# First group's z from the unscaled input, and the state-space rounds rearranged

## The reference, cut to what matters

```python
u = rmsnorm(h, mix_norm)
z   = in_cols(u, w_in, 5)                                    # 2048 wide
xbc = silu(causal_conv(in_cols(u, w_in, 6), conv_w, conv_b)) # 4 taps; x 2048, B 1024, C 1024
dt  = softplus(in_cols(u, w_in, 7) + dt_bias)                # 32 heads
# 8 groups, 4 heads each, head width 64, state 128, chunks of 64 tokens; da = dt * a
cum = cumsum(da); seg = cum[t] - cum[s]; decay = exp(where(s <= t, seg, -inf))
cb = C B^T; y = (cb * decay) (x*dt) + exp(cum) * (C state)
state = exp(cum_last) * state + B^T (x * dt * exp(cum_last - cum))
y = (y + D * x) * silu(z)
y = rmsnorm(y) per group of 256 channels, * ssm_norm         # then the branch's output matrix
```

## Time and profile before

| | |
|---|---|
| median of 3 runs | 1847.29 us (1846.7 to 1848.17) |
| profiled execution | 1847.36 us |
| its span, first to last instruction | 1845.5 us |
| TensorE busy (matmuls) | 98% |
| VectorE, ScalarE, GpSimd busy | 53%, 33%, 8% |
| granted TensorE clock, mean | 0.995 of full speed |

### The profile page before, as it was taken

The page is one execution under the profiler, slowest core; times in us unless marked ns, Lnnn a source line. Parts: engine busy times, 40 slices in busy tenths (PEclk is TensorE's granted clock), DMA queues, the critical chain, the costliest instruction groups (busy, mean ns, idle before and its releaser), DMA issues.

```text
span 1845.5 us, 26225 instructions
## 1 busy us (share of the span) xinstructions
PE 1806.9 (98%) x9852; PEld 1508.4 (82%) x9852; DVE 977.6 (53%) x1376; ACT 610.7 (33%) x942; POOL 145.1 (8%) x116
## 2 busy tenths in 40 slices
PE   7999999999999999999999999999999999999997
PEld 5888888878888888788988888887888888888885
DVE  6444443379888888732444445545334544444333
ACT  4323222233333344332233334443222422323221
POOL 4111100031111111100000000000000011111000
PEclk9999999999999999999999999999999999999998
DMA  4323223322222222132222222222222322223331
GB/s 154 103 93 100 93 101 103 110 84 70 73 74 69 68 68 68 58 103 91 92 69 82 90 87 82 84 78 89 95 99 91 103 92 92 101 92 101 103 105 66
DMA packets 47352, 164.91 MB, mean 89 GB/s; under 512 B 5520, under 2 KB 6672, under 8 KB 47296
## 3 DMA queue, kind: packets, MB, share of 16 engines
q1 hardware_dynamic: 43584, 158.10, 26.1%
q10 hardware_dynamic: 3712, 6.03, 1.0%
HBM read 162.01 MB, written 2.10 MB: 89 GB/s over the span
## 4 chain that ended last, share of the span: by engine, by line
PE 70%; issue 21%; DVE 6%; POOL 1%; ACT 1%; DMA 0%; DVEq 0%; POOLq 0%; ACTq 0%; SPq 0%
PE G L534 33%; PE G L576 12%; PE I L534 9%; PE G L550 7%; DVE WL L1443 2%; DVE CV L1626 1%; PE I L896 1%; POOL hid L456 1%; PE I L930 1%; PE I L906 1%; PE I L704 1%; PE I L712 1%; PE G L761 1%; DVE UL L1459 1%; DVE un L1581 1%
## 5 line engine op out<-in xcount | busy, mean ns | idle before, releaser
L1443 DVE TENSOR_TENSOR WL<-RAW,WH 128x1024 fp32r<-128x1024 f32 x297 | 387.9, 1309 | 298.2 <-ACT WH L1025 290.2
L1025 ACT CAST WH<-RAW 128x1024 fp32r<-128x1024 f32 x297 | 309.6, 1048 | 230.9 <-PE I L534 126.2
L534 PE MATMUL G<-UH,WH 128*128 128x512 f32 x696 | 172.8, 390 | 0.0
L534 PE MATMUL G<-UH,WL 128*128 128x512 f32 x696 | 171.9, 389 | 0.0
L534 PE MATMUL G<-UL,WH 128*128 128x512 f32 x696 | 171.9, 389 | 0.0
L534 PEld LDWEIGHTS G<-UH,WH 128*128 128x128 f32 x696 | 130.6, 188 | 28.0 <-issue 1.0
L534 PEld LDWEIGHTS G<-UH,WL 128*128 128x128 f32 x696 | 130.6, 188 | 27.1
L534 PEld LDWEIGHTS G<-UL,WH 128*128 128x128 f32 x696 | 130.6, 188 | 27.1
L534 PE MATMUL G<-NH,WH 128*128 128x512 f32 x448 | 113.2, 395 | 1.4 <-ACT SC L1098 1.4
L534 PE MATMUL G<-NL,WH 128*128 128x512 f32 x448 | 110.7, 389 | 0.0
L534 PE MATMUL G<-NH,WL 128*128 128x512 f32 x448 | 110.6, 389 | 0.0
(11 more groups left out here) (299 smaller groups left out, 2477.5 us busy)
## 6 DMA issues: line engine op xcount, KB each, us to landing
RAW<-in_slabs SPq DMA_DIRECT2D x297, 512.0 KB, 3.3
h<-in_x SPq DMA_DIRECT2D x4, 512.0 KB, 6.8
bias<-in_rel ACTq DMA_DIRECT2D x16, 128.0 KB, 3.0
out_y<-h ACTq DMA_DIRECT2D x8, 256.0 KB, 2.2
bias<-in_rel ACTq DMA_DIRECT2D x16, 112.0 KB, 2.6
cst<-in_cst SPq DMA_DIRECT2D x1, 168.0 KB, 3.6
ut<-in_wgk SPq DMA_DIRECT2D x3, 32.0 KB, 8.8
```

What stands on the lines that cost most here:

```text
L534: ins = mm(dst, W[:, n.slot, (k - k0) * P:(k - k0 + 1) * P], R[:, k, :], start=begin and which == 0 and k == k0, stop=end and which == 2 a ...
L1025: nc.scalar.copy(WH[:, n.slot, :], RAW[:, n.slot, :]).then_inc(split_hi, 1)
L1443: V.tensor_tensor(WL[:, n.slot, :], RAW[:, n.slot, :], WH[:, n.slot, :].bitcast(F32), ALU.subtract).then_inc(split_lo, 1)
```

## The change

- Group 0's z tile is computed from UH and UL. ScalarE evicts it with the token's 1/rms as a scale (`raw_z`), takes tanh from SBUF, VectorE gates it there. The sums of dt (`dt_sums`) follow z instead of standing between its third and fourth block, and write to I34.
- NL is made by VectorE (`scaled_lo`), four tiles behind `dt_logits` and four behind `dt_softplus`; `raw_evict` and `conv_begin` of tile 0 stand earlier, and the order of what VectorE and ScalarE do up to group 0's end is new.
- MSH (`da_hi`) and MSL (`da_lo`) read SC directly instead of gsc, and those of group g + 1 are made in round g: MSH behind `conv_silu` of tile 3, MSL behind `intra` of group g.
- XD is made on ScalarE already multiplied by D, in four activations (one a head); XTE and XDT are computed from I01 itself, XTE first, ahead of `lo`. GpSimd's multiplication goes.
- `conv_silu` and `ssm_y` change places: Y stands behind the silu of tile 2. One `hi` moves behind BK's copy, the squares move ahead of tanh 3.
- The squares have 1/256 in their scale; the variance is an addition on GpSimd; ScalarE scales two of Y's four blocks, VectorE two.
- `ssm_intra` takes the two halves of the partitions in turn for each head, instead of four heads of one half, then four of the other.

```diff
@@ GpSimd
             def da_lo(g):
-                pool.wait_ge(sems["group_const"], after("group_const", g))
                 pool.wait_ge(sems["intra_done"], last("intra_done", g - 1))
-                inc(nc.gpsimd.tensor_tensor(MSL[:].rearrange("p (q t) -> p q t", t=CH),
-                                            bc(gsc[:, 28:32, :].rearrange("p j r -> p (j r)"), CH),
-                                            causal[:].unsqueeze(1).to_broadcast([P, TT * HPG, CH]), ALU.mult),
+                inc(nc.gpsimd.tensor_tensor(MSL[:].rearrange("p (j r t) -> p j r t", j=TT, t=CH),
+                                            bc(SC[:, 28:32, bass.ds(HPG * g, HPG)], CH), causal_all, ALU.mult),
                     "da_lo_masked")
             def ssm(g):
-                pool.wait_ge(sems["xte_ready"], after("xte_ready", g))
-                pool.wait_ge(sems["group_norm"], after("group_norm", g))
-                d = ggrp[:, 2:6].unsqueeze(1).unsqueeze(3).to_broadcast([P, TT, HPG, CH])
-                x4 = XD[:].rearrange("p j (r c) -> p j r c", r=HPG)
-                inc(nc.gpsimd.tensor_tensor(x4, x4, d, ALU.mult), "xd_ready")
+                pool.wait_ge(sems["ssm_squares"], last("ssm_squares", g))
...
+                inc(nc.gpsimd.tensor_tensor(var4[:], ss4[:], four_eps[:], ALU.add), "ssm_var")
                 pool.wait_ge(sems["ssm_var"], after("ssm_var", g))
                 inc(nc.gpsimd.tensor_tensor(rstd4[:], var4[:], minus_half[:], ALU.pow), "ssm_rstd")
...
             norm(1)
-            for m in range(KT):
-                pool.wait_ge(uh_ready, 16 + m + 1)
-                nc.gpsimd.tensor_tensor(NL[:, m, :], un[:, m, :], NH[:, m, :].bitcast(F32),
-                                        ALU.subtract).then_inc(ul_ready, 1)
             da_split()
-            with pool.Fori(0, NG) as i:
-                da_lo(i)
+            pool.wait_ge(dt_pool, DA_SPLIT)
+            pool.wait_ge(ul_ready, 24)
+            da_lo(0)
+            with pool.Fori(0, NG - 1) as i:
+                da_lo(i + 1)
                 ssm(i)
+            ssm(NG - 1)
@@ TensorE
                 pe.wait_ge(sems["da_lo_masked"], last("da_lo_masked", g))
+                pe.wait_ge(dt_act, 6)
...
                 pe.wait_ge(sems["xte_ready"], after("xte_ready", g))
+                pe.wait_ge(sems["xdt_ready"], after("xdt_ready", g))
...
             def ssm_intra():
-                for c in range(NCH):
-                    j, s = c // 2, half(c)
+                for j in range(TT):
                     for rr in range(HPG):
-                        ins = mm(I01[s, j * 256 + rr * CH:j * 256 + (rr + 1) * CH], M[s, j, rr, :],
-                                 XDT[s, j, rr * CH:(rr + 1) * CH], start=True, stop=True)
+                        for s in (half(0), half(1)):
+                            ins = mm(I01[s, j * 256 + rr * CH:j * 256 + (rr + 1) * CH], M[s, j, rr, :],
+                                     XDT[s, j, rr * CH:(rr + 1) * CH], start=True, stop=True)
...
+            for j in range(TT):
+                tm_tile(n + 4, wn + 4, j, source=(UH, UL))
+            dt_sums()
             pe.wait_ge(uh_ready, 24)
             pe.wait_ge(ul_ready, 24)
-            for j in range(TT):
-                tm_tile(n + 4, wn + 4, j)
-                if j == 2:
-                    dt_sums()
-            pe.wait_ge(dt_act, 6)
@@ ScalarE
+            def raw_z(n, wn):
+                act.wait_ge(slab_done, n.value + 2)
+                act.wait_ge(norm_rstd, 2)
+                for j in range(TT):
+                    bank = (wn + j // 2).slot
+                    ins = A(ZS[:, j, :], G[:, bank, (j % 2) * 256:(j % 2 + 1) * 256], ACT.Copy, scale=rstd4[:, j:j + 1])
+                    ins.then_inc(z_scaled, 1)
+                    if j % 2:
+                        act.wait_ge(z_scaled, j + 1)
+                        act.sem_inc(g_free[bank], 1)
...
-                inc(nc.scalar.copy(XD[:].rearrange("p j c -> p (j c)"), I01[:]), "x_copied")
+                act.wait_ge(sems["group_norm"], after("group_norm", g))
+                for rr in range(HPG):
+                    ins = A(XD[:, :, rr * CH:(rr + 1) * CH],
+                            I01[:].rearrange("p (j c) -> p j c", j=TT)[:, :, rr * CH:(rr + 1) * CH], ACT.Copy,
+                            scale=ggrp[:, 2 + rr:3 + rr])
+                inc(ins, "x_copied")
...
+            def ssm_scale(g):
+                act.wait_ge(sems["ssm_rstd"], last("ssm_rstd", g))
+                for j in range(TT // 2):
+                    inc(A(Y[:, j, :], Y[:, j, :], ACT.Copy, scale=rstd4[:, j:j + 1]), "ssm_scaled_act")
...
                 hi(n + 5)
+                hi(n + 6)
                 conv_begin(0, 2, n + 2, wn + 2)
                 conv_tanh(0, 1, wn + 1)
-                hi(n + 6)
                 conv_begin(0, 3, n + 3, wn + 3)
+                raw_z(n + 4, wn + 4)
+                hi(n + 7)
+                decay_exps()
+                conv_tanh(0, 2, wn + 2)
+                hi(n + 8)
+                conv_tanh(0, 3, wn + 3)
...
                 for t in range(4):
-                    conv_begin(p, t, n + t, wn + t)
+                    conv_begin(p, t, n + t, wn + t, t > 0)
                     if t == 0:
-                        ssm_copy_exp(inner)
+                        ssm_copy_exp(inner, n + 3)
+                    if t == 3:
+                        ssm_squares(inner)
                     conv_tanh(p, t, wn + t)
-                ssm_squares(inner)
+                ssm_scale(inner)
@@ VectorE
                 lo(At(N_SMALL + 4))
                 raw_evict(1, n + 1, wn + 1)
+                dt_logits()
+                for m in range(4):
+                    scaled_lo(m)
+                conv_taps(0, 0, n, wn)
+                raw_evict(2, n + 2, wn + 2)
+                lo(n + 4)
+                lo(n + 5)
+                dt_reciprocal()
+                conv_silu(0, 0)
+                conv_taps(0, 1, n + 1, wn + 1)
+                raw_evict(3, n + 3, wn + 3)
+                lo(n + 6)
+                dt_softplus()
+                for m in range(4, KT):
+                    scaled_lo(m)
...
                 conv_silu(0, 1)
                 conv_taps(0, 2, n + 2, wn + 2)
-                lo(n + 6)
                 conv_silu(0, 2)
+                dve.wait_ge(dt_pool, DA_SPLIT)
+                da_hi(0)
+                lo(n + 7)
                 conv_taps(0, 3, n + 3, wn + 3)
                 conv_silu(0, 3)
+                dt_to_end()
+                group_scalars(0)
+                lo(n + 8)
...
                 for t in range(4):
                     conv_taps(p, t, n + t, wn + t)
-                    lo(n + t + 3)
                     if t == 0:
                         ssm_x(inner)
+                    lo(n + t + 3)
                     if t == 1:
                         ssm_m(inner)
                         ssm_chain(inner)
-                    if t == 3:
+                    conv_silu(p, t)
+                    if t == 2:
                         ssm_y(inner)
-                    conv_silu(p, t)
+                da_hi(p)
                 ssm_scale(inner)
```

More of the change, by code:

```diff
@@ L565, in fm_fresh, with tm_tile @@
                 ins.then_inc(slab_done, 1)
-            def tm_tile(n, wn, j, thirds=range(3)):
+            def tm_tile(n, wn, j, thirds=range(3), source=(NH, NL)):
                 if j == 0 and thirds[0] == 0:
@@ L652, in dt_sums @@
                 da = SC[:, 0:4, :].rearrange("p j h -> p (j h)")
-                mm(I01[:, T:T + 128], upto_t[:], da, start=True, stop=True)
-                mm(I01[:, T + 128:T + 256], after_s[:], da, start=True, stop=True)
+                mm(I34[:, 0:128], upto_t[:], da, start=True, stop=True)
+                mm(I34[:, 128:256], after_s[:], da, start=True, stop=True)
                 for c in range(NCH):
-                    dst = I2[:, 32 * (c // 2):32 * (c // 2) + 32] if c % 2 else \
-                        I01[:, T + 256 + 16 * c:T + 288 + 16 * c]
-                    ins = mm(dst, ones[half(c), :], SC[half(c), c // 2, :], start=True, stop=True)
+                    o = (T if c % 2 else 256) + 32 * (c // 2)
+                    ins = mm(I34[:, o:o + 32], ones[half(c), :], SC[half(c), c // 2, :], start=True, stop=True)
                 ins.then_inc(dt_pe, 1)
@@ L716, in turn_back @@
             def turn_back(src, dst, ready, g, done):
-                pe.wait_ge(sems[ready], last(ready, g))
+                for name in ready:
+                    pe.wait_ge(sems[name], last(name, g))
                 for f in range(2):
@@ L797, in _ @@
                     0: lambda: ssm_turn(i), 1: lambda: ssm_cb_u(i), 3: lambda: (ssm_inter(i), ssm_intra()),
-                    7: lambda: turn_back(Y, I01, "ssm_scaled", i, "ssm_turned")})
+                    7: lambda: turn_back(Y, I01, ("ssm_scaled", "ssm_scaled_act"), i, "ssm_turned")})
             g = NG - 1
@@ L809, in _ @@
             output_half(n + 3, wn + 3, 0)
```

(23 more changed lines are left out.)

82 lines of the change are left out of this document (40 added, 42 removed).

## The result

The changed kernel took 1851.3 us, the kernel before 1847.18, each the median of 18 runs: a ratio of 1.0021 with an interval of [1.0014, 1.0028]. So it is 4 us slower, where 1836.5 was forecast, and it lies outside the range. One of the 18 runs before took 3666.69 us, which the median does not feel. The profiled execution has a span of 1848.5 us.

A forecast was written before the change was run, and what follows sets the result against it. With TensorE busy for 98% of the span, only its waits, lower-clock stretches and time between matmuls could be won. Terms 1.3 + 6.7 + 1.4 + 1.4 = 10.8 us off the median 1847.29 gave 1836.5, range 1833 to 1840.

The forecast's parts named there:

- rival 4: Y scaled too late, so turn_back stalls 1.8 us in each of 8 groups: 14.5 us, above 1851; chance 0.06.
- Rival 3: turn_back becomes the wait because GpSimd's operations keep VectorE's: 0.3 to 1.2 us a round, 1839 to 1845; chance 0.14.
- rival 5: The waits go and others of the same size come in, so no change; chance 0.02.
- 43.6 to 43.9 named for right: Sign that the forecast is right: the state-space rounds take 43.6 to 43.9 us each.
- Group 0: First state-space group: gap before z goes, a 4.3 us wait comes before XT's transposes; 1.3 us gained, bounds -1.2 and 5.5.
- warm or cold: Group 0: u cannot start before XTE and XDT are ready at 439.8, whether TensorE's clock is full or low.
- the taps could be kept back: Group 0's lower bound of -1.2 us: silu 1 or taps 2 kept back 2.5 us by GpSimd's MSL.
- The rounds: Rounds after group 0: the MSL and XTE waits go, 6 x 1.12 = 6.7 us, bounds 0 and 6.7.
- `turn_back` holds: End of each round: scaled Y ready at 42.5, wanted at 43.15, margin 0.65 us; no stall booked, up to 1.2 a round.
- `intra`: the term: Alternating halves in intra gives back 3 to 4 ns an instruction: 8 x 0.18 = 1.4 us, bounds 0 and 10.5.
- rival 1: The two halves of intra overlap, worth 10.5 us: time 1828.5; chance 0.10.
- The last group: Last state-space group: X products ready 0.7 us earlier, inter 1.2 to 2.2 earlier; 1.4 us gained, bounds 0.5 and 3.

The follow-up runs named there:

- e7: The changed kernel with four_eps in the unused half of minus_half's 32 bytes, so every tensor lies where it lay before the change: 1833.92 us, ratio 0.9925.
- e1: The kernel before with an unused 16-byte tensor where four_eps would stand: 1863.62 us, ratio 1.009.
- e9: e7 with group 0's conv chain put earlier in the queues of VectorE and ScalarE: 1832.47 us, ratio 0.992.
- e8: e7 with intra in its old order, four heads of one half, then four of the other: 1838.94 us, ratio 0.9951.
- e4: The kernel before with the weight buffers WH and WL moved by 32 bytes and everything behind them by 64: 1878.85 us, ratio 1.0173.
- e2: The kernel before with an unused tensor of 64 bytes where four_eps would stand: 1846.06 us, ratio 0.9991.
- e3: The changed kernel with 16 unused bytes behind four_eps, so the tensors behind it move by 64: 1835.24 us, ratio 0.9933.

## Why the prediction was wrong, point by point

**The step that failed** is one that the working did not even list, and so priced at nothing: the tensor `four_eps`, and with it the assumption that matmuls which the change does not touch keep their pace. (The working says it once, of "TensorE's fm ends unchanged until 407.28", and there it held, because those products are on UH and UL.) The trace of before could not show the price, for in it every distance was a multiple of 512. In its place the runs show 17.4 us (e7 against the changed kernel) or 16.2 (e1 against the kernel before), from the distance between the two operands of each matmul. That took the forecast 10.8 us and the 2.5 more that the change brings, and left 4 of loss. The time lies where rival 4 put it, above 1851, but its mechanism is not there: `turn_back` waits in no round. Rival 3 is out for the same reason, and rival 5, no change, because e7 is 13.3 faster. One sign was met by luck: the changed kernel's rounds take 517.23 - 473.54 = 43.69 us, within the 43.6 to 43.9 named for right. There the shorter `intra` made up for the slower matmuls.

The rest is read against e7, where the layout is that of before. Its feed-forward started 0.82 later than before by the trace (258.97 against 258.15), so 0.82 comes off its times. Its timeline in group 0:
```profile
421.16 2.11 PE L536 MATMUL G<-NH,WH 128*128 128x512 f32 x8
...
431.27 1.73 PE L668 MATMUL I<-ident,XT 128*128 128x128 f32 x8 [4.36 <-DVE CT L1703]
...
435.17 2.01 PE L536 MATMUL G<-NH,WH 128*128 128x512 f32 x8
...
440.74 0.69 PE L686 MATMUL I<-CT,BT 128*64 128x64 f32 x16
441.35 1.13 PE L693 MATMUL I<-XTE,BK 64*128 64x256 f32 x8
442.32 1.02 PE L698 MATMUL I<-XTE,BK 64*128 64x256 f32 x6
443.27 2.12 PE L536 MATMUL G<-NH,WH 128*128 128x512 f32 x8
```
**Group 0: right in its waits, 0.8 instead of 1.3.** Round 0 begins at 420.34, forecast 420.35. The stall is 4.36, forecast 4.3. XTE and XDT are there at 439.85, forecast 439.8:
```profile
439.46 1.21 DVE L1725 TENSOR_TENSOR XDT<-I,gsc 128x1024 f32<-128x1024 f32 x1
```
But u comes at 440.53, 0.7 later, and is over at 442.45, where 441.8 to 442.0 was forecast and 443.25 was read before. No wait stands in front of it: TensorE itself was late. From the first transposes to the next fm it took 3.90 us at a clock of 0.54, against 2.27 at the full clock in e9. So the lower clock cost 1.6 us, and the step "warm or cold" was wrong: 0.9 or so went into the time in which u would have waited for XDT, and the other 0.7 were lost.

The conv chain itself kept its forecast, tanh 2 done at 423.58 for 423.6, although raw_z took 1.78 for 1.6 and taps 2, which the walk priced undisturbed at 2.23, ran beside GpSimd's MSL. The row is VectorE's of the changed kernel:
```profile
421.59 3.95 DVE L1684 SCALAR_TENSOR_TENSOR CV<-BT,gconv,CV 128x511 f32<-128x511 f32 x3
```
MSL ran from 421.20 to 423.43 there. That the taps could be kept back was named as a bound; tanh 2 did not wait for them, since ScalarE still had the exponentials to do when they ended.

**The rounds: right.** The chain of e7, with z of rounds 0 and 1:
```profile
456.33 2.01 PE I L707 x64
458.34 11.71 PE G L578 x96
...
501.66 11.71 PE G L578 x96
```
A round takes 501.66 - 458.34 = 43.32 where it took 45.06: 1.74 less, of which 0.61 is `intra` and 1.13 the two waits (1.12 forecast). Six rounds give 6.8.

**`turn_back` holds.** The forecast feared GpSimd beside VectorE. In round 1 of the changed kernel, whose first fm is at 473.54, VectorE and GpSimd show:
```profile
506.17 1.82 DVE L1769 TENSOR_TENSOR Y<-Y,XD 128x1024 f32<-128x1024 f32 x1
...
514.27 0.61 DVE L1777 TENSOR_SCALAR Y<-Y,rstd 128x256 f32<-128x256 f32 x2
```
```profile
505.01 1.91 POOL L437 TENSOR_TENSOR MSL<-SC,causal 128x1024 fp32r<-128x1024 f32 x1 [34.59 <-PE I L707]
511.79 0.88 POOL L446 TENSOR_TENSOR var<-ss,four_eps 128x4 f32<-128x4 f32 x1 [4.88 <-ACT ssm_dump L1163]
512.75 1.33 POOL L448 TENSOR_TENSOR rstd<-var,minus_half 128x4 f32<-128x4 f32 x1
```
Y<-Y,XD overlaps MSL for 0.75 us and is 0.6 longer. Y<-Y,I, whose second operand lies in PSUM, ran beside the same MSL in its usual 1.22. MSL took 1.91 where 3.0 was allowed, so the last product into Y is finished at 35.7 of the round (36.8 forecast) and VectorE's half of Y is scaled at 41.3 (42.5). The addition took 0.88 (0.9 forecast); the power 1.33 beside VectorE's work, where it took 1.01 before with VectorE idle, and both are hidden. By the Trainium skill ("GPSIMD Engine Reference", Specifications) the two engines share their SBUF interfaces for instructions with two SBUF inputs; the trace agrees, with the 0.6 us and the 1.22 above.

**`intra`: the term was mis-sized, 4.9 instead of 1.4, and its mechanism was wrong.** The profile has two records for each of the 32 products. The 64 take 2.01 us, 31 ns each on average, where 37 to 38 were taken from L870, and e8 confirms the term as 5.0. The prediction compared such averages with the 27 ns that it gave 64 columns, and read them as one record after the other. The starts of single records say otherwise. In the kernel before, the last four of round 0, all of one half, start at 458.54, 458.60, 458.65 and 458.71, 58 ns apart. In the changed kernel records start in pairs, 6 to 7 ns apart, and a pair follows the last one after 58: 32 pairs make 1.9 of the 2.01 us. So the two halves do run at the same time, which is the mechanism of rival 1. Its 10.5 us did not come because the old order overlapped in part as well: without any overlap 64 records would take 3.7 us (an estimate from the 58), and they took 2.62. L870, the witness against rival 1, was misread: its records come in pairs too, 216 ns from pair to pair. u in the timeline of e7 above shows the same without single records. Four products in alternating halves, eight records, take 442.32 - 441.35 = 0.97 us; the three products behind them, six records, take 0.95, because the last has no partner in the other half: its two records start at 442.75 and 442.97, 216 ns apart. The Trainium skill ("TensorE: Matmul & The Clock Gate", Part 3: Packing small matmuls) has matmuls of different row groups start about 4 ns apart; the trace agrees, with its 6 to 7 ns. The Trainium skill ("TensorEngine Tiling (Array Packing)", Restrictions and Gotchas) keeps row tiles from using one PSUM bank at once; by that rule the term would be 0, and the trace differs: both halves write one bank, each in its own partitions, and overlap all the same.

**The last group: 0.8 instead of 1.4.** In e7 u comes at 741.96, after waits of 1.41 for BK and 1.28:
```profile
740.00 0.69 PE L686 MATMUL I<-CT,BT 128*64 128x64 f32 x16 [1.41 <-ACT BK L1153]
741.96 1.96 PE L693 MATMUL I<-XTE,BK 64*128 64x256 f32 x8 [1.28 <-issue]
...
766.92 1.06 PE L725 MATMUL I<-ident,Y 128*128 128x128 f32 x8 [0.70 <-ACT Y L1174]
```
Counted from the group's first fm (730.60 in e7, 741.63 before), u comes at 11.36 instead of 11.86, 0.5 earlier where 0.7 was forecast: XTE waits for the four XD copies, which stand behind `hi` on ScalarE, and XDT behind XTE. But `inter` comes only 0.7 earlier (20.54 for 21.27), not 1.2 to 2.2. No wait stands in front of it any more (it had waited 0.33 for SS); what is late is TensorE itself, since u ran at the lower clock again. In e9, behind the same two waits but at the full clock, u is over 1.6 sooner and `inter` comes at 19.23, 2.0 earlier. So the forecast is right for an execution that keeps the clock, and the step that failed in e7 is that u's cold run was left out. To the long run of merge products behind the group (774.41 in e7, 786.89 before, in the chains) 1.45 are gained, 0.61 of them in `intra`.

The terms are thus 0.8 + 6.8 + 4.9 + 0.8 = 13.3, and 1847.18 - 1833.92 = 13.3 was measured between before and e7; less the 17.4 for the layout, that is the loss of about 4.

**Open.** Why the distance matters was not shown, nor why matmuls on the unmoved SH are slower behind a group that is off. Distances of 160 to 448 were not tried; 480 is UH in e4, 32 short of a multiple. The 256-column matmuls, whose best distance is another one, took 11.12 us for z's 96 in e2 and 11.52 in e3 at the same distance of 64; that stays unexplained.

## What to carry to other kernels

A new tensor is never free only because it is small: look at what is allocated behind it, and compare the pace of long back-to-back runs of matmuls in code that the change does not touch, before looking for waits. If a part that ends before the first changed instruction is slower, suspect the layout, and test it with an unused tensor of the same size in the old kernel. When a stall on a shared queue goes, list what that queue still owes before the next wait; e9 removed a stall of 4.4 us and got 0.3 in that group. And before an average per instruction is taken to mean that nothing overlaps, look at the starts of single records, with one stretch in which nothing can overlap as the measure.

## What the runs showed of the hardware

The pace of back-to-back fp32r matmuls of 512 columns depends on the distance in SBUF between moving and stationary operand: 226.7 ns at multiples of 512 bytes (the layout of before), 233.3 at 32, 96 and 128 more and at 32 less, 228.9 at 64 more, with a granted clock of 1.00 in the down projections of before and of the changed kernel. In a kernel that is TensorE for 98%, 32 bytes are worth 16.2 us, and 31 where all products are hit (e4). Products of 64 rows in the two halves of the partitions run at the same time: their records start 6 to 7 ns apart, while two records in one half are 58 ns apart for 64 columns and 216 for 256. Behind the same wait of 1.28 us the granted clock fell to 0.53 in e7 and stayed at 1.00 in e9; u and what follows took 1.6 us longer for it. Three taps on VectorE took 3.95 us beside GpSimd's MSL and 2.31 without, and a GpSimd power of 128x4 took 1.33 beside VectorE and 1.01 alone.
